# Gated projections in pieces behind one conditioning block each, and seven products per weight block for the values of latent and context

## The chip, the core and the metric

One core of a Trainium2 chip runs the whole program. Its engines work side by side: TensorE multiplies matrices, VectorE and ScalarE work element by element, GpSimd does what is left to it, SyncE issues most transfers from memory. The metric is the time of one execution on the device in microseconds. Everything is float32.

## What is computed

Two transformer layers in a row over 256 tokens of width 1024. The change lies at the start of the first. Cut to what matters there:

```python
mod_lat = silu(c)     @ w_ada + b_ada          # conditioning, 6 x 1024 columns
mod_ctx = silu(c_ctx) @ w_ada + b_ada
u_ctx = h_ctx * (1 + csc_m) + csh_m            # 256 tokens of context
u_lat = h_lat * (1 + sc_m) + sh_m              # 256 tokens of latent
k_c, v_c = split(u_ctx @ w_in[:, K_OFF:G_OFF])             # k 1024, v 2048 columns
q, k, v, g, glu, gates = split(u_lat @ w_in)
# q and k are turned by rope; o = retention of q over k, v and over k_c, v_c in both directions
za, zb = split(glu); z = za * sigmoid(zb)      # gated projection, then a convolution of 31 taps
z = silu(layernorm(depthwise_conv(z)))
mix = (sigmoid(ga) * (silu(g) * head_norm(o)) @ w_ret_out + sigmoid(gb) * (z @ w_conv_out)) @ w_mix_out
h = layernorm(ALPHA * h_lat + gt_m * mix)      # then experts, then the second layer
```

## The kernel before, in words

Activations lie with the width on the 128 partitions and the tokens along the free dimension: `uT` (latent) and `ucT` (context) are eight tiles of 128x256. Weights come in blocks of 1024 rows by 512 columns, 2048 KB, into eight bays. Three bays are the `ring`; the others are tensors that are free at the time: RA, Vc, KQ, ZC, and `extra` with a bit of uT. `make_jobs` lists the loads and the TensorE jobs of each block; a load waits until the last job on its bay is done, and `ROUNDS` and `EARLY_BAYS` say which bay is next. SyncE issues the loads in this order, one after the other.

At the start come four conditioning blocks (`ada`). For each, TensorE multiplies the two conditioning vectors by it (L783), VectorE copies the row (L1296), TensorE turns it to columns (L840) and VectorE adds the bias (L1267, L1271). Matmuls that compute nothing (L821) stand in the gaps. `ADA_FIRST` sets the order so that two blocks give the shift and the scale of half of the width. ScalarE (`modulate`, L510) and VectorE (L1303) then make `uT`. The first gated block is a `deep_job` (L832), whose sum runs over the width in the outer loop; the other three are ordinary jobs (L794). Their results go to two PSUM buffers of four tiles each (`PP`, a "pair"), used in turn; ScalarE takes the sigmoid, VectorE multiplies (L1347) and writes `zpad`. After each of them VectorE does 16 taps of the convolution (`convolve`, L1333 for the first tap of a tile, L1335 for the rest), each on 128x256 elements, each behind a wait on the one before.

Then k for latent and context, q, and the rope on VectorE (L1356 to L1358). The values: for each of four weight blocks one job for the context and one for the latent, 2 x 8 matmuls of 512 columns each (L805), into a pair; VectorE adds the bias (`with_bias`, L1364), then does 16 taps. TensorE may be one job ahead. GpSimd issues the transfers of the bias rows (L476) and computes nothing there. The last tap is followed by a reduction over the channels (L1340). In the heads behind it, PSUM tensors `MB0` to `MB3` take the scores (L896) and the outputs (L910, L913), and eight more conditioning blocks are multiplied, one per head.

## Time and profile before

| | us |
|---|---|
| median of 3 runs (1511.61 to 1511.84) | 1511.73 |
| the profiled execution itself | 1514.14 |
| its span, first to last instruction | 1512.3 |
| TensorE busy | 1463.0 |
| VectorE busy | 490.9 |
| ScalarE busy | 226.7 |
| GpSimd busy | 17.8 |

How to read it: a busy time is the sum of an engine's instructions in the profiled execution, which has a time of its own, here 2.4 us above the median. A float32 matmul appears as two instructions ("passes"), so that 16 of them are 8 matmuls. Passes are pipelined: their own duration overlaps that of the next, and the spacing of starts is what one costs. PE is TensorE, PEld its load of stationary operands, DVE is VectorE, ACT ScalarE, POOL GpSimd, SP SyncE.

### The profile page before, as it was taken

The numbers are of one execution on the slowest core, as the hardware profiler recorded it, in microseconds if no ns is written. First come the engines' busy times: TensorE is split into PE (matmuls) and PEld (weight loads), VectorE is DVE, ScalarE is ACT, GpSimd is POOL, SyncE is SP. The second block draws the span as 40 slices with busy tenths as digits, with TensorE's granted clock in tenths as the row PEclk, the third lists the DMA queues.
The fourth block names the chain that finished last, engine by engine and source line by source line (L and its number), as shares of the span: only waits on it lengthen the run. The fifth ranks groups of instructions, "written<-read, shape, count | busy, mean of one in ns | idle before, by whom it ended". The sixth has DMA issues, their size and how long they took to land.

```text
span 1512.3 us, 19230 instructions
## 1 busy us (share of the span) xinstructions
PE 1463.0 (97%) x8282; PEld 941.3 (62%) x8282; DVE 490.9 (32%) x1060; ACT 226.7 (15%) x438; POOL 17.8 (1%) x38
## 2 busy tenths in 40 slices
PE   8999999999999999999999998999999999999996
PEld 6888644564688887555555444445788886455542
DVE  1637866643102135223222121214223252211122
ACT  1210300231213004201111010112121022111011
POOL 0000000000000010000000000000010000000000
PEclk9999999999999999999999999999999999999999
DMA  9623322583434486999999999997564747999985
GB/s 388 271 86 112 112 83 105 184 317 132 156 127 163 169 354 241 371 427 428 427 426 427 428 427 428 428 421 322 144 224 158 281 167 289 429 426 428 427 336 249
DMA packets 36184, 435.42 MB, mean 288 GB/s; under 512 B 4336, under 2 KB 5752, under 8 KB 9736
## 3 DMA queue, kind: packets, MB, share of 16 engines
q1 hardware_dynamic: 33264, 427.89, 69.6%
q0 software_dynamic: 1664, 4.52, 0.8%
q10 hardware_dynamic: 1176, 1.84, 0.8%
q8 instruction: 63, 1.03, 0.3%
q14 instruction: 17, 0.14, 0.0%
HBM read 431.61 MB, written 2.62 MB: 287 GB/s over the span
## 4 chain that ended last, share of the span: by engine, by line
PE 83%; DMA 15%; DVE 1%; issue 1%; ACT 0%; SPq 0%; POOL 0%; DVEq 0%; POOLq 0%
PE PP L794 26%; PE PP L1069 17%; PE PP L805 12%; PE PP L1084 9%; PE MB L1053 5%; DMA ZC<-in_w_moe 5%; PE PP L832 4%; DMA RA<-in_w_moe 2%; DMA ring<-in_w_moe 2%; DMA Vc<-in_w_moe 2%; DMA uT<-in_w_moe 2%; PE PP L1045 1%; DMA Vc<-in_w_ada 1%; PE MB L910 1%; PE PP L783 1%; PE MB L896 1%
## 5 line engine op out<-in xcount | busy, mean ns | idle before, releaser
L794 PE MATMUL PP<-uT,ring 128*128 128x256 f32 x960 | 208.8, 379 | 0.0
L794 PEld LDWEIGHTS PP<-uT,ring 128*128 128x128 f32 x960 | 182.0, 190 | 25.1 <-issue 0.5
L805 PE MATMUL PP<-ring,uT 128*128 128x512 f32 x288 | 125.1, 593 | 0.0
L1335 DVE SCALAR_TENSOR_TENSOR ZC<-ZC,vec 128x256 f32<-128x256 f32 x240 | 116.4, 485 | 8.6
L1069 PE MATMUL PP<-ring,const 128*64 128x256 f32 x992 | 112.1, 380 | 5.1 <-DMA ring<-in_w_moe 4.8
L1053 PE MATMUL MB<-V 64*128 64x512 f32 x400 | 112.4, 640 | 1.7 <-DVE V L1718 0.9
L1697 DVE TENSOR_SCALAR V<-V 128x1 f32<-128x1 f32 x50 | 7.7, 154 | 309.2 <-PE PP L1069 309.2
L1069 PEld LDWEIGHTS PP<-ring,const 128*64 128x64 f32 x992 | 72.2, 137 | 49.0 <-issue 11.6
L805 PEld LDWEIGHTS PP<-ring,uT 128*128 128x128 f32 x288 | 54.4, 190 | 67.6 <-issue 67.6
L1712 DVE SCALAR_TENSOR_TENSOR V<-V 128x256 f32<-128x256 f32 x100 | 48.5, 485 | 108.7 <-PE MB L1053 94.0
L1084 PE MATMUL PP<-ring,const 128*64 128x512 f32 x336 | 76.7, 598 | 0.1
L658 ACT ACTIVATE V<-PP 128x256 f32<-128x256 f32 x50 | 19.2, 383 | 379.3 <-PE PP L1069 379.3
L1069 PE MATMUL PP<-ZC,const 128*64 128x256 f32 x512 | 58.3, 380 | 6.5 <-DMA ZC<-in_w_moe 6.3
L1069 PE MATMUL PP<-RA,const 128*64 128x256 f32 x512 | 58.3, 380 | 4.1 <-DMA RA<-in_w_moe 3.9
L662 ACT ACTIVATE const<-small 128x512 f32 x50 | 31.8, 636 | 168.2 <-PE PP L1069 167.8
L805 PE MATMUL PP<-ring,RA 128*128 128x512 f32 x128 | 55.6, 592 | 0.0
L794 PE MATMUL PP<-Vc,ring 128*128 128x256 f32 x256 | 55.6, 379 | 0.0
L1069 PEld LDWEIGHTS PP<-ZC,const 128*64 128x64 f32 x512 | 36.6, 137 | 29.1 <-DMA ZC<-in_w_moe 9.0
L1069 PEld LDWEIGHTS PP<-RA,const 128*64 128x64 f32 x512 | 36.6, 137 | 28.5 <-DMA RA<-in_w_moe 8.4
L794 PEld LDWEIGHTS PP<-Vc,ring 128*128 128x128 f32 x256 | 48.6, 190 | 6.6
L1084 PEld LDWEIGHTS PP<-ring,const 128*64 128x64 f32 x336 | 22.3, 136 | 47.0 <-issue 45.1
L1053 PEld LDWEIGHTS MB<-V 64*128 64x128 f32 x400 | 30.3, 184 | 30.4 <-issue 30.1
(399 smaller groups left out, 1641.9 us busy)
## 6 DMA issues: line engine op xcount, KB each, us to landing
ring<-in_w_moe SPq DMA_DIRECT2D x54, 2048.0 KB, 18.7
RA<-in_w_moe SPq DMA_DIRECT2D x22, 2048.0 KB, 16.0
ZC<-in_w_moe SPq DMA_DIRECT2D x22, 2048.0 KB, 17.4
KQ<-in_w_moe SPq DMA_DIRECT2D x18, 2048.0 KB, 18.7
Vc<-in_w_moe SPq DMA_DIRECT2D x17, 2048.0 KB, 18.4
extra<-in_w_moe SPq DMA_DIRECT2D x17, 1792.0 KB, 16.5
ring<-in_w_ada SPq DMA_DIRECT2D x11, 2048.0 KB, 8.4
ring<-in_w_gates SPq DMA_DIRECT2D x7, 2048.0 KB, 7.8
```

Of the source, the lines that this page charges most:

```text
L658: nc.scalar.activation(sg, bank[0][:, 0:L], ACT.Silu).then_inc(m["sg_ready"], 1)
L662: nc.scalar.activation(xs, xsc[:, :, bass.ds(at, SLOTS)], ACT.Copy).then_inc(m["xs_ready"], 1)
L783: ins = pe.matmul(out[at:at + 32, 0:2, :].rearrange("p a n -> p (a n)"), x, W[:, k * 512:(k + 1) * 512], start=k < 4 and late <= 0, stop=k ...
L794: ins = pe.matmul(out[:, c, :], W[:, k * width + at:k * width + at + P], X[:, k, :], start=k == 0, stop=k == K - 1)
L805: ins = pe.matmul(out[:, 2 * t:2 * t + 2, :].rearrange("p a n -> p (a n)"), X[:, k, t * P:(t + 1) * P], W[:, k * 512:(k + 1) * 512], start ...
L832: ins = pe.matmul(out[:, c, :], W[:, k * 512 + c * P:k * 512 + (c + 1) * P], X[:, k, :], start=k == 0 and c % 2 == 0, stop=k == DT - 1 and ...
L896: ins = pe.matmul(out[:, m, :], keys[:, h, m * P:(m + 1) * P], qT[:, h, :], start=True, stop=True)
L1053: ins = pe.matmul(acc[t][g], S[rows, t * P:(t + 1) * P], ys[rows, :], start=first, stop=done == "acc_done", tile_position=(SLOTS * g, 0))
L1069: ins = pe.matmul(bank[q][SLOTS * g:SLOTS * (g + 1), 0:L], x[:, k, :], weights(W, k * 512 + g * 256, 256), start=k == 0, stop=k == DT - 1, ...
L1084: ins = pe.matmul(bank[2][SLOTS * g:SLOTS * (g + 1), :], hts[:, c % 2, SLOTS * (c // 2):SLOTS * (c // 2 + 1)], weights(W, c * D + g * 512, ...
L1335: ins = V_.scalar_tensor_tensor(conv[:, t, :], zpad[:, t, k:k + L], tap, conv[:, t, :], ALU.mult, ALU.add)
L1712: linked(V_.scalar_tensor_tensor(Sk[:, c], placer[:, c], slotcol, weightr[:, c], ALU.is_equal, ALU.mult), k, c + 2)
```

## The change

Gated blocks 0 to 2 come in four pieces (`w_piece`), each with two of the eight width tiles of all three blocks, 1536 KB. The columns of the first four conditioning blocks are put in another order, so that block b gives shift and scale of width tiles 2b and 2b + 1. Behind conditioning block b these two tiles of `uT` are made, one by ScalarE and one by VectorE, and `glu_piece` adds their part to the sums of all three gated blocks, which stay open in both pairs and in MB2 and MB3. The conditioning rows use MB0 and MB1. The fourth gated block is one job as before. The context is loaded when the pieces are done.

The values of latent and context are one product of a 2 x 2 matrix (latent or context by halves of the width) with a 2 x 2 matrix (halves of the width by halves of the block's columns). `seven_products` computes it by seven products of quarters in place of eight. Five sums of quarters of the inputs are made once, five sums of quarters of the weights for each block, all on GpSimd. The results go to MB0 to MB3 in turn, and VectorE adds each to one or two quarters of V and Vct (`add_product`). Between the products VectorE does 3 or 4 taps; two taps and the reduction are left for the time behind the first g block. Bay 0 holds the weight sums, so that the value blocks come into bays 1 and 2 alone.

```diff
@@ make_jobs
-ADA_FIRST = (0, 2, 1, 3)
-EARLY_BAYS = (0, 1, 2, 4, 5)
+PIECES = 4
+EARLY_BAYS = (0, 1, 0, 1, 2, 4, 5, 3, 0, 1, 2, 0, 1, 2, 1, 2, 1)
+SUM_BAY = 0
...
-    order = (("mix1", (("ada", 4, ["ada"]), ("glu", 4, ["cm8"]), ("k", 2, ["cm8", "cm8c"]),
-                       ("q", 2, ["cm8"]), ("v", 4, ["tm8c", "tm8"]), ("ada", 8, ["ada"]), ("g", 4, ["tm8"]), ("gates", 4, ["cm8"]),
+    order = (("mix1", (("ada", 4, ["ada"]), ("piece", PIECES, []), ("glu", 4, ["cm8"]), ("k", 2, ["cm8", "cm8c"]),
+                       ("q", 2, ["cm8"]), ("v", 4, ["seven"]), ("ada", 8, ["ada"]), ("g", 4, ["tm8"]), ("gates", 4, ["cm8"]),
...
+        u_sums = [kw, Pc] + [extra[:, D * i:D * (i + 1)].rearrange("p (a n) -> p a n", a=4) for i in range(3)]
+        w_sums = [ring[:, SUM_BAY, D * i:D * (i + 1)].rearrange("p (a n) -> p a n", a=4) for i in range(4)] + [raw]
...
+        def quarters(b):
+
+            W = bays[loads[J["v", b, 0]["w"]]["bay"]].rearrange("p (k n) -> p k n", n=512)
+            return W[:, 0:4, 0:256], W[:, 0:4, 256:512], W[:, 4:8, 0:256], W[:, 4:8, 256:512]
+        lat1, lat2, ctx1, ctx2 = uT[:, 0:4, :], uT[:, 4:8, :], ucT[:, 0:4, :], ucT[:, 4:8, :]
@@ GpSimd
+            pool.wait_ge(u_ready, PIECES + 1)
+            pool.wait_ge(u_second, PIECES)
+            for out, x, y, op in zip(u_sums, (ctx1, lat1, lat1, ctx1, lat2), (ctx2, lat2, ctx2, lat1, ctx2),
+                                     (ALU.add, ALU.add, ALU.add, ALU.subtract, ALU.subtract)):
+                nc.gpsimd.tensor_tensor(out, x, y, op).then_inc(sums_made, 1)
+            job_wait(pool, J["q", 0, 0])
+            for b in range(4):
+                w_wait(pool, J["v", b, 0]["w"])
+                B11, B12, B21, B22 = quarters(b)
+                for i, (x, y, op) in enumerate(((B12, B22, ALU.subtract), (B21, B11, ALU.subtract), (B11, B22, ALU.add),
+                                                (B11, B12, ALU.add), (B21, B22, ALU.add))):
+                    if b:
+                        seven_wait(pool, b - 1, i + 2)
+                    elif i == 4:
+                        pool.wait_ge(rope_done, 4)
+                    nc.gpsimd.tensor_tensor(w_sums[i], x, y, op).then_inc(sums_made, 1)
@@ TensorE
+            def glu_piece(q, b):
+
+                if b == 0:
+                    w_wait(pe, piece[q])
+                    pe.wait_ge(u_ready, q + 1)
+                    pe.wait_ge(u_second, q + 1)
+                W = bays[loads[piece[q]]["bay"]]
+                for k in (2 * q, 2 * q + 1):
+                    for c in range(4):
+                        at = (2 * b + k % 2) * 512 + c * P
+                        ins = pe.matmul(glu_at(b, c), W[:, at:at + P], uT[:, k, :], start=k == 0 and c % 2 == 0,
+                                        stop=k == DT - 1 and c % 2 == 1)
...
-            deep_job(J["glu", 0, 0], uT, {0: first_half, 4: second_half})
-            for b in range(1, 4):
-                job(J["glu", b, 0])
+            for q in range(PIECES):
+                glu_piece(q, 0)
+                if q + 1 < PIECES:
+                    first_ada(q + 1)
+                glu_piece(q, 1)
+                if q + 1 < PIECES:
+                    turn_ada(q + 1)
+                glu_piece(q, 2)
+            job(J["glu", 3, 0])
...
+            def seven_products(b):
+
+                B11, _, _, B22 = quarters(b)
+                made = len(u_sums) + len(w_sums) * b
+                for p, (x, y, sums) in enumerate(((u_sums[0], B11, 1), (u_sums[1], B22, 2), (lat1, w_sums[0], made + 1),
+                                                  (ctx2, w_sums[1], made + 2), (u_sums[2], w_sums[2], made + 3),
+                                                  (u_sums[3], w_sums[3], made + 4), (u_sums[4], w_sums[4], made + 5))):
+                    n = 7 * b + p
...
+                    pe.wait_ge(sums_made, sums)
+                    if n >= 4:
+                        pe.wait_ge(seven_kept, n - 3)
+                    for t in range(LT):
+                        for k in range(4):
+                            ins = pe.matmul(MB[n % 4][:, t, :], x[:, k, t * P:(t + 1) * P], y[:, k, :], start=k == 0, stop=k == 3)
@@ VectorE
-            for h in range(2):
-                decay(h)
-                context_decay(h)
+            def add_product(b, p):
...
+                if p < 2:
+                    dve.wait_ge(bias_full[b % 2], 16 * (b // 2 + 1))
+                    plus, minus = ((ctx[0], bias[0]), (ctx[1], bias[1])) if p == 0 else ((lat[1], bias[1]), (lat[0], bias[0]))
+                    V_.tensor_tensor(plus[0], M, plus[1], ALU.add)
+                    ins = V_.scalar_tensor_tensor(minus[0], M, -1.0, minus[1], ALU.mult, ALU.add)
+                else:
+                    for out in ((lat[1], ctx[1]), (ctx[0], lat[0]), (lat[0], ctx[1]), (ctx[1],), (lat[0],))[p - 2]:
+                        ins = V_.tensor_tensor(out, out, M, ALU.add)
+                say(dve, ins, seven_kept, n + 1)
+            step = 9 * A_JOB
             for b in range(4):
-                with_bias(J["v", b, 0], b, Vct[:, :, b * 512:(b + 1) * 512])
-                convolve((9 + 2 * b) * A_JOB, (10 + 2 * b) * A_JOB)
-                with_bias(J["v", b, 1], b, Vt[:, :, b * 512:(b + 1) * 512])
-                convolve((10 + 2 * b) * A_JOB, (11 + 2 * b) * A_JOB)
+                for p in range(7):
+                    add_product(b, p)
+                    taps = 3 if p < 2 or b == 3 and p > 4 else 4
+                    convolve(step, step + taps)
+                    step += taps
+                if b < 2:
+                    for h in range(2):
+                        (decay, context_decay)[b](h)
...
+                if b == 0:
+                    convolve(step, DT * TAPS)
```

TensorE at the start of the program, before. `sT` holds the conditioning vectors; the line numbers are those of the kernel before:

```order
L783 MATMUL PP<-ring,sT 32x512 x8
L840 MATMUL PP<-lead,small 128x2 x4
L821 MATMUL MB<-V 128x128 x5
L783 MATMUL PP<-Vc,sT 32x512 x8
L840 MATMUL PP<-lead,small 128x2 x4
L821 MATMUL MB<-V 128x128 x6
L832 MATMUL PP<-uT,KQ 128x256 x32
L794 MATMUL PP<-uT,ring 128x256 x128
```

These are the third and the fourth conditioning block, then the first gated block; the last row is the other three gated blocks and k's first job. The same engine and place in the changed kernel, from the first conditioning block on (L906 is the conditioning job, L914 the turning, L928 a piece, L858 an ordinary job):

```order
L906 MATMUL MB<-ring,sT 32x512 x8
L885 MATMUL MB<-V 128x128 x3
L914 MATMUL MB<-lead,small 128x2 x4
L885 MATMUL MB<-V 128x128 x6
L928 MATMUL PP<-uT,ring 128x256 x8
L906 MATMUL MB<-ring,sT 32x512 x8
L928 MATMUL PP<-uT,ring 128x256 x8
L914 MATMUL MB<-lead,small 128x2 x4
L928 MATMUL MB<-uT,ring 128x256 x8
L928 MATMUL PP<-uT,Vc 128x256 x8
```

The gated matmuls now begin behind the first conditioning block, and each later conditioning job and turning stands between two of them. VectorE in the value stage before, one block of the four (L1364 adds the bias, L1335 and L1333 are taps):

```order
L1364 TENSOR_TENSOR V<-PP,biasr 128x2x512
L1335 SCALAR_TENSOR_TENSOR ZC<-ZC,vec 128x256 x16
L1364 TENSOR_TENSOR Vc<-PP,biasr 128x2x512
L1335 SCALAR_TENSOR_TENSOR ZC<-ZC,vec 128x256 x8
L1340 TENSOR_REDUCE rs<-ZC 128x256
```

The same in the changed kernel, the first five products of a block (L1498 and L1499 start the values with the bias, L1502 adds, L1431 and L1429 are taps):

```order
L1498 TENSOR_TENSOR Vc<-MB,biasr 128x2x256
L1499 SCALAR_TENSOR_TENSOR Vc<-MB,biasr 128x2x256
L1431 SCALAR_TENSOR_TENSOR ZC<-ZC,vec 128x256 x3
L1498 TENSOR_TENSOR V<-MB,biasr 128x2x256
L1499 SCALAR_TENSOR_TENSOR V<-MB,biasr 128x2x256
L1431 SCALAR_TENSOR_TENSOR ZC<-ZC,vec 128x256 x3
L1502 TENSOR_TENSOR V<-V,MB 128x2x256
L1502 TENSOR_TENSOR Vc<-Vc,MB 128x2x256
L1431 SCALAR_TENSOR_TENSOR ZC<-ZC,vec 128x256 x4
```

In place of one addition of 1024 elements for 16 taps there are one or two of 512 for 3 or 4 taps. GpSimd in the changed kernel, where before only the transfers of the bias rows stood (L516 makes sums of the inputs, L527 of the weights):

```order
L508 DMA biasr<-in_bias_rows 128x512 x2
L516 ISA
L516 TENSOR_TENSOR small<-RA 128x1024
L516 TENSOR_TENSOR small<-uT 128x1024
L516 TENSOR_TENSOR extra<-uT,RA 128x1024
L516 TENSOR_TENSOR extra<-RA,uT 128x1024
L516 TENSOR_TENSOR extra<-uT,RA 128x1024
L527 TENSOR_TENSOR ring<-ring 128x1024 x4
L527 TENSOR_TENSOR small<-ring 128x1024
```

Five sums of the inputs come first, then five of the first weight block; the row of four and the one behind it come three more times.

## Rows read from the trace of the kernel before

**Rows 1.** The page, busy us with share and instructions, and the granted clock.

```profile
PE 1463.0 (97%) x8282; PEld 941.3 (62%) x8282; DVE 490.9 (32%) x1060; ACT 226.7 (15%) x438; POOL 17.8 (1%) x38
...
PEclk9999999999999999999999999999999999999999
```

**Rows 2.** The chain of waits, first 300 us: start us, us, what.

```profile
2.60 20.73 DMA Vc<-in_w_ada
...
29.99 14.05 PE PP L832 x64
44.05 124.32 PE PP L794 x576
168.37 109.87 PE PP L805 x256
278.23 1.74 PE MB L896 x8
...
280.10 0.69 DVE small L1410
280.79 0.61 DVE small L1412
```

**Rows 3.** Order of time, conditioning stage: start, us, engine, line, operation [idle before].

```profile
9.11 1.92 PE L783 MATMUL PP<-ring,sT 128*32 128x512 f32 x16 [1.71 <-DMA ring<-in_w_ada]
...
11.17 0.69 DVE L1296 COPY small<-PP 128x512 f32<-128x512 f32 x1 [11.17 <-PE PP L783]
...
11.91 1.05 PE L840 MATMUL PP<-lead,small 128*128 128x2 f32 x8 [0.88 <-DVE small L1296]
...
13.07 0.23 DVE L1267 TENSOR_TENSOR modT<-PP,lead 128x4 f32<-128x4 f32 x2 [1.22 <-PE PP L840]
...
14.12 1.92 PE L783 MATMUL PP<-ring,sT 128*32 128x512 f32 x16
...
28.90 0.17 DVE L1271 TENSOR_SCALAR modT<-modT 128x8 f32<-128x8 f32 x1
29.11 1.09 ACT L510 ACTIVATE uT<-hT,modT 128x256 f32<-128x256 f32 x2 [0.80 <-DVE modT L1271]
```

**Rows 4.** Order of time, context on ScalarE and the first gated block on VectorE.

```profile
45.25 4.04 ACT L510 ACTIVATE RA<-RA,modT 128x256 f32<-128x256 f32 x8 [6.85 <-DMA RA<-in_ctxT]
...
51.59 0.88 DVE L1347 SCALAR_TENSOR_TENSOR ZC<-PP,vec,small 128x256 f32<-128x256 f32 x2 [9.24 <-ACT small L528]
```

**Rows 5.** Busy time in the value stage: stretch, its length, each engine, clock, DMA.

```profile
168.20:278.20 110.00, 110.00 (x258) 48.77 (x257) 75.97 (x133) 10.04 (x17) 1.61 (x3) 1.00 0.23 84
```

**Rows 6.** Order of time, VectorE in the value stage.

```profile
177.99 0.75 DVE L1381 SCALAR_TENSOR_TENSOR small<-const,lgs 128x512 f32<-128x512 f32 x1
...
184.31 0.69 DVE L1387 TENSOR_TENSOR small<-small 128x512 f32<-128x512 f32 x1 [0.35 <-ACT small L565]
184.92 1.22 DVE L1364 TENSOR_TENSOR Vc<-PP,biasr 128x1024 f32<-128x1024 f32 x1
...
197.19 8.30 DVE L1335 SCALAR_TENSOR_TENSOR ZC<-ZC,vec 128x256 f32<-128x256 f32 x16
...
270.02 3.67 DVE L1340 TENSOR_REDUCE rs<-ZC 128x256 f32<-128x2048 f32 x1
```

**Rows 7.** Order of time, the one GpSimd operation on tensors, at the span's end.

```profile
1507.87 1.26 POOL L497 TENSOR_TENSOR Kc<-Kc,uT 128x512 f32<-128x512 f32 x1 [342.77 <-ACT Kc L765]
```

**Rows 8.** What writes Kc at the end: durations ns min/median/max, first and last start.

```profile
L1770 DVE SCALAR_TENSOR_TENSOR Kc<-MB,biasr,uT x3: 742/742/752, 1507.0 to 1508.4; 128x512 f32<-128x512 f32 x3
```

**Rows 9.** Order of time, the second late conditioning block on TensorE.

```profile
290.66 1.92 PE L783 MATMUL PP<-ring,sT 128*32 128x512 f32 x16
```

**Rows 10.** DMA issues, 230 to 350 us: count, KB each, median us to landing.

```profile
ring<-in_w_ada SPq DMA_DIRECT2D x7, 2048.0 KB, 8.1
```

More of the change, by code:

```diff
@@ L112, in make_jobs @@
             first = sum(x["src"] == src for x in loads)
-            for b in ADA_FIRST if src == "ada" and not first else range(first, first + count):
+            for b in range(first, first + count):
                 for half, kind in enumerate(kinds):
                     jobs.append(dict(src=src, b=b, kind=kind, half=half, w=len(loads), i=len(jobs), pair=dense % 2, use=dense // 2))
-                    dense += src != "ada" or b < 4 or b == 11
-                loads.append(dict(src=src, b=b, bay=bay_of(phase)))
+                    dense += (src != "ada" or b == 11) and (src, b) != ("glu", 2) and src != "v"
+                    if src == "glu" and b < 3:
+                        jobs[-1]["w"] -= 1
+                if src != "glu" or b == 3:
+                    loads.append(dict(src=src, b=b, bay=bay_of(phase)))
         experts(n)
     last_of = {j["w"]: j["i"] for j in jobs}
+    pieces = [w for w, x in enumerate(loads) if x["src"] == "piece"]
+    last_of |= {w: last_of[pieces[-1]] for w in pieces}
     for w, x in enumerate(loads):
@@ L122, in make_jobs @@
         x["nth"], x["prev"] = len(before), before[-1] if before else None
+    last_v = next(w for w, x in enumerate(loads) if (x["src"], x["b"]) == ("v", 3))
+    next(x for x in loads[last_v + 1:] if x["bay"] == SUM_BAY)["prev"] = last_v
     return jobs, {(j["src"], j["b"], j["half"]): j for j in jobs}, loads, last_of
@@ L346, in tail_bays, with glu_at, seven_wait @@
             return [order[(done + q) % len(order)] for q in range(3)]
+        piece = [w for w, x in enumerate(loads) if x["src"] == "piece"]
+        def glu_at(b, c):
+            return MB[2 + c // 2][:, c % 2, :] if b == 2 else PP[J["glu", b, 0]["pair"]][:, c, :]
+        def seven_wait(eng, b, p):
+            if p == 6:
+                eng.wait_ge(job_done, J["v", b, 0]["i"] + 1)
+            else:
+                eng.wait_ge(seventh, 6 * b + p + 1)
+        def quarters(b):
+            W = bays[loads[J["v", b, 0]["w"]]["bay"]].rearrange("p (k n) -> p k n", n=512)
+            return W[:, 0:4, 0:256], W[:, 0:4, 256:512], W[:, 4:8, 0:256], W[:, 4:8, 256:512]
+        lat1, lat2, ctx1, ctx2 = uT[:, 0:4, :], uT[:, 4:8, :], ucT[:, 0:4, :], ucT[:, 4:8, :]
         def job_wait(eng, j):
@@ L407, in _ @@
             sp.dma_start(lead[:, :], a["lead"]).then_inc(ld_c, 16)
-            for w in range(4):
-                load(w)
-            sp.dma_start(hT[:, :, :], a["xT"]).then_inc(ld_x, 16)
-            for half, done in enumerate((ld_glu, w_full[loads[4]["bay"]])):
-                h = slice(half * BLK // 2, (half + 1) * BLK // 2)
-                sp.dma_start(bays[loads[4]["bay"]][:, h], a["w_glu"][0, :, h]).then_inc(done, 16)
+            load(0)
+            sp.dma_start(hT[:, 0:2, :], a["xT"][:, 0:2, :]).then_inc(ld_x, 16)
+            load(piece[0])
+            load(1)
+            sp.dma_start(hT[:, 2:8, :], a["xT"][:, 2:8, :]).then_inc(ld_xs, 16)
+            load(piece[1])
+            load(2)
+            load(piece[2])
+            load(3)
+            load(piece[3])
             sp.dma_start(vec[:, :], a["vec"]).then_inc(ld_vec, 16)
-            sp.wait_ge(w_full[loads[2]["bay"]], 16)
+            load(8)
             sp.dma_start(row[:, :], a["rows"].partition_broadcast(P)).then_inc(ld_rest, 16)
             sp.dma_start(const[:, :], a["const"]).then_inc(ld_rest, 16)
-            load(5)
+            load(9)
+            job_wait(sp, J["glu", 2, 0])
             sp.dma_start(ctxT, a["ctxT"]).then_inc(ld_ctx, 16)
-            for w in range(6, at[0]):
-                if w == 8:
+            for w in range(10, at[0]):
+                if w == 12:
                     sp.dma_start(wr[0][:, :, :], a["wr0"]).then_inc(ld_wr, 16)
@@ L538, in raw_copy @@
                 else:
-                    act.wait_ge(pair_free[1], J["glu", 3, 0]["use"] + 1)
+                    last = J["glu", 3, 0]
+                    act.wait_ge(pair_free[last["pair"]], last["use"] + 1)
                 for i in range(4):
@@ L781, in job @@
                         at, late = 32 * (k % 4), j["b"] - 4
[L782 to L784 removed]
+                        ins = pe.matmul(out[at:at + 32, 0:2, :].rearrange("p a n -> p (a n)"), sT[:, k, 8 - late:40 - late],
+                                        W[:, k * 512:(k + 1) * 512], start=k < 4 and late == 0, stop=k >= 4 and late == 7,
+                                        tile_position=(0, at))
                 elif kind in ("cm8", "cm8c", "cm4", "cm16"):
@@ L876, in _ @@
                 job(J["k", b, 0])
[L877 removed]
+                pe.wait_ge(u_ready, PIECES + 1)
                 job(J["k", b, 1])
```

157 lines of the change are left out of this document (88 added, 69 removed).

## The prediction

> **What bounds the kernel now.** I read the page's busy shares first, then the chain of waits of the first 300 us, the order of time on each engine around it, and the DMA issues. TensorE is busy 97% of the span, at a granted clock of 9 tenths or more in every slice [rows 1] and 1.00 in the value stage [rows 5], so the higher of its two levels, 2.4 GHz. In the chain [rows 2] the reader is to see two parts. Until 29.99 us the conditioning blocks come in by DMA and TensorE has next to nothing to do. From there to 278.2 us there is only TensorE: 14.05 us for the first gated block, nine jobs of 124.32 / 9 = 13.81 us (three gated, four k, two q), eight value jobs of 109.87 / 8 = 13.73 us. So a piece of TensorE work taken away here is worth its time, as long as VectorE (busy 75.97 of 110 us in the value stage [rows 5]) and the transfers keep up. The kernel after 278 us is the same program; its loads are released by TensorE's jobs and move with them.
>
> **Part 1, gated projections in pieces.** Before, TensorE computes nothing of the projections until all four conditioning blocks have come, 2048 KB each, one per 14.12 - 9.11 = 5.01 us [rows 3]. The change puts a quarter of the rows' depth of three gated blocks (1536 KB) behind each conditioning block. At 2.5 us per 1024 KB: the first block lands at 9.1 us as now, x's first two tiles at 9.7, piece 0 at 13.5, conditioning block 1 at 18.5, and each further pair 8.8 us later (a little more at first, for the rest of x: 20.4).
>
> TensorE: conditioning job 0 ends at 9.1 + 1.92 = 11.0; copy 0.69 (+0.14), turning 1.05, VectorE's sum 0.23 and 0.17 with their gaps, then one tile modulated on ScalarE in 1.09 / 2 = 0.55 [rows 3]: about 14.2, behind piece 0. One (piece, block) is 16 passes, 13.81 / 4 = 3.45 us, so TensorE works to 17.7 and waits until 18.5. From there I find no wait: conditioning jobs 1 to 3 at 1.87, eleven more quarter jobs 38.0, three turnings at 0.93 (their spacing in the dense stretch), the fourth gated block 13.8: 18.5 + 5.6 + 38.0 + 2.8 + 13.8 = 78.7. Conditioning block 2 is asked for at about 31.7 and lands at 29, block 3 at 45.5 and lands at 38: from the second piece on the margin grows. Before, the same point is 44.05 + 3 x 13.81 = 85.5. **Gain 6.7 us.** If the transfers came 20% slower the loss would be at the first two waits only, about 3 us.
>
> What is late next: VectorE. Gated block 0 now finishes at 58 (after the last piece), not 44, then come four rounds of 0.88 + 16 taps of 0.519 = 9.2 us [rows 4, 6]. Block 3 leaves PSUM at 87.4; the first context job of k needs that buffer at 78.7 + 13.8 = 92.5. Margin 5 us. The context is asked for after the pieces (it lies where piece 3 lay): 65 + 5 + 4.04 us on ScalarE [rows 4] = 74, needed at 92.5. So T, the start of the value stage, goes from 168.4 to 161.7.
>
> **Part 2, seven products.** Removed: 8 jobs, 109.87 us. Added: 4 x 7 products of 2 x 4 matmuls of 256 columns, 16 passes each: 28 x 3.45 = 96.7 us. TensorE alone gains 13.1 us. The additions that pay for it lie on two other engines.
>
> VectorE: 20 products have two additions out of PSUM, 8 have one. No row shows this form at 512 elements on V; the nearest is L1410 with L1412 behind it, 0.69 and then 0.61 [rows 2]; half of the 1024-element form, 1.22 / 2 = 0.61, is the lower end and 0.75 (L1381) the upper [rows 6]. I take 0.69 + 0.61 + 0.04 = 1.34 for two, 0.73 for one: 32.6 us. Taps 102 x 0.519 = 52.9, four decay steps and two sums 4.5. Together 90.0 us. A product has 1.34 + 4 x 0.519 = 3.42 us of VectorE against 3.45 of TensorE. That is no slack at all, but VectorE may lag four products (n waits for n - 4). It comes free at T + 9.6 (the rope ends at 177.96 [rows 6]), so product 0 leaves at T + 11.0 and is needed at T + 13.8; by the same count the margin stays above 2 us through the stage. At the end VectorE is at T + 9.6 + 90.0 = T + 99.6, plus 0.69 for the first score operation = T + 100.3. Before it was 280.79 - 168.37 = T + 112.4 [rows 2]. So 1.1 of the 13.1 us are given back and **12.1 us** gained; at the lower end of the addition 1 us more, at the upper 2.5 less.
>
> GpSimd: 5 sums of the inputs and 20 of weight quarters, 128x1024 each. The only such row is L497, 1.26 us for 512 elements [rows 7]. Bounds: 1.26 if all of it were fixed, 2.52 if it goes with the size; I take 2.4. Five per block are 12 us of its 24.2, and every sum may start when the product that used it last is over, a block ahead: hidden, unless one took over 4.8 us. The first four for block 0 have 13.8 + 6.9 us for 9.6.
>
> What these sums do to VectorE beside them is the one open price, since no row shows a GpSimd operation that reads beside a VectorE operation with two tensors out of SBUF, which a tap is. Bounds: nothing, and the whole of each sum, 2.4 us. The nearest row is L1770, three operations of 742, 742 and 752 ns, of which the latter two ran beside L497 [rows 7, 8], so at nothing or 0.01 us. I take nothing. It is a near row, not an equal one: L1770 takes one tensor from PSUM.
>
> On this the Trainium skill speaks against the change. "SBUF — State Buffer", section "Who interferes with whom", says that a VectorE instruction with two SBUF inputs contends with a GpSimd one that reads SBUF, and that whichever is first keeps the shared ports for its whole length, while one with a single SBUF input is left alone. L1770 agrees with the second half; on the first no row here bears. By it the sum is that of rival A.
>
> Elsewhere: in the heads behind the values, conditioning load 2 of the late eight is now asked for at the stage's end and not a block earlier (its bay holds the weight sums). It lands in 8.1 us and is used 290.66 - 278.23 = 12.4 us in [rows 2, 9, 10]: free; without those 4 us it would cost what is missing. The last two taps and the reduction, 1.0 + 3.67 us [rows 6], move behind the first g block, where a job of 13.73 us of TensorE covers them beside two operations of 1.22 us.
>
> **Sum.** The profiled execution took 1514.14 us with a span of 1512.3. 6.7 + 12.1 = 18.8 off, with 0.8 put back for the additions' upper end: 1496.1 for it. It stood 2.4 us above the median of the runs, so **1493.7 us** for that.
>
> **Rivals.**
> A. Each sum stops VectorE for its whole length. Price: the four sums before T fall on rope and taps, 9.6 us; of the stage's 90 us of VectorE work 57.4 (64%) read two tensors from SBUF, so the 16 other sums cost between 0.64 x 38.4 = 24.6 and 38.4 us, take 31.5. The end is T + 141.4, 29 us later than before. In part 1 the five input sums, 12 us, exceed the margin of 5 us: TensorE waits 7 us for the PSUM buffer, which eats its gain. Together +29 us: **1541**. For it: a tap has two SBUF tensors, and VectorE has no slack. Against it: only that the near row shows nothing. It decides from 18.8 / 20 = 0.94 us per sum upward: below that the kernel is still faster.
> B. In between: the two engines slow each other for part of the time, 0.3 to 1.2 us per sum. 20 x that against 18.8: 1499 to 1517, take **1506**.
> C. The change doesn't reach what it says: the stage's pace is set by VectorE because the additions take 1.5 and 0.8 us with their waits. 20 x 0.16 + 8 x 0.07 = 3.8 us: **1498**. Nothing in the rows speaks for it.
>
> **How the numbers follow.** Forecast, with C as its edge: 0.42 (1490 to 1499). B 0.20, of it 0.10 faster, 0.03 the same, 0.07 slower. A 0.34 (1525 to 1555), since what speaks against it is a row of another form. A late transfer or another stall of over 19 us: 0.04, slower. Faster 0.52, same 0.03, slower 0.45; within 0.2% (3 us) a measurement can't tell a change from none. The likeliest case is 1493.7, its own range 1490 to 1499; the range of 8 in 10 has to reach into A: 1490 to 1543.
>
> **What would show it.** Part 1: TensorE dense from 18.5 us, one wait before it, fourth gated block over at 78.7; wrong if it waits for a piece or for PSUM at 92. Part 2: 448 passes at 0.216 us in 97 us without a wait for VectorE's additions. The taps beside GpSimd's sums: 485 ns in the forecast, some of them 2.5 us and more in A, where TensorE's waits name the additions. The score stage starts at about T + 97 in the forecast, past T + 130 in A. The forecast is wrong if the taps' mean rises above some 0.6 us.

## The result, and the profile after

The changed kernel takes **1538.03 us** (median of 4 runs, 1537.36 to 1538.96) against 1511.78 for the kernel before (4 runs, 1511.61 to 1513.39). The ratio is 1.017, with a 95% interval of 1.0157 to 1.0183: slower by 26 us. The forecast of 1493.7 was wrong, and so was its direction. The time that came is near that of rival A, 1541; the wide range of 1490 to 1543 holds it only because it was stretched to reach into A.

From the page of the changed kernel: busy us with share and instructions (as in [rows 1]), then the shares of each engine in the chain of work that ended last, then the row of the taps (busy us and mean ns behind the first bar).

```profile
PE 1458.8 (95%) x8450; PEld 978.2 (64%) x8450; DVE 556.7 (36%) x1102; ACT 227.4 (15%) x438; POOL 79.0 (5%) x63
...
PE 70%; DMA 14%; DVE 14%; issue 1%; ACT 0%; SPq 0%; POOL 0%; DVEq 0%; POOLq 0%
...
L1431 DVE SCALAR_TENSOR_TENSOR ZC<-ZC,vec 128x256 f32<-128x256 f32 x240 | 154.2, 643 | 8.6
```

VectorE now holds 14% of the chain that ended last; before it was 1%. The taps have a mean of 643 ns; before it was 485, and 16 of them with their gaps took 8.30 us [rows 6]. A mean hides what happened; the spread of the same line does not (durations ns min/median/max):

```profile
L1431 DVE SCALAR_TENSOR_TENSOR ZC<-ZC,vec x240: 483/485/2725, 62.7 to 382.8; 128x256 f32<-128x256 f32 x120
```

The median tap is what it was. A few take five times as long. The chain of waits in the first block of the value stage (start us, us, what) shows which, with GpSimd's order of time in the same stretch under it:

```profile
189.48 0.69 DVE Vc L1498
190.17 0.61 DVE Vc L1499
190.78 0.02 issue
190.81 1.37 DVE ZC L1431
192.18 0.02 issue
192.20 2.47 DVE ZC L1431
194.67 0.02 issue
194.69 2.46 DVE ZC L1431
197.16 0.02 issue
197.18 0.69 DVE V L1498
197.87 0.61 DVE V L1499
```
```profile
189.53 2.35 POOL L527 TENSOR_TENSOR small<-ring 128x1024 f32<-128x1024 f32 x1 [21.67 <-DVE KQ L1457]
191.84 5.03 POOL L527 TENSOR_TENSOR ring<-ring 128x1024 f32<-128x1024 f32 x2
197.58 2.35 POOL L527 TENSOR_TENSOR ring<-ring 128x1024 f32<-128x1024 f32 x1 [0.72 <-PE MB L980]
```

GpSimd's sum of 189.53 to 191.88 runs beside two additions out of PSUM (L1498, L1499), which take 0.69 and 0.61 us, as costed. The tap that starts at 190.81 ends only at 192.18, 0.30 us after the sum. The next two taps take as long as the next two sums (5.03 us for both). In these rows a sum stops a tap, which reads only SBUF, and leaves alone an addition that reads PSUM beside one SBUF tensor, which is what L1770 was [rows 8].

Where TensorE then waits (start us, us, ..., in brackets the idle time before and what ended it), in part 1, in the value stage and in front of the second head's scores:

```profile
20.34 1.92 PE L906 MATMUL MB<-ring,sT 128*32 128x512 f32 x16 [2.44 <-DMA ring<-in_w_ada]
...
67.07 26.28 PE L858 MATMUL PP<-uT,ring 128*128 128x256 f32 x121
...
100.33 16.17 PE L858 MATMUL PP<-RA,ring 128*128 128x256 f32 x64 [5.47 <-DVE ZC L1443]
...
171.59 7.07 PE L980 MATMUL MB<-ring,small 128*128 128x256 f32 x32
...
190.92 6.58 PE L980 MATMUL MB<-ring,extra 128*128 128x256 f32 x16 [5.36 <-DVE Vc L1499]
...
297.74 1.10 PE L997 MATMUL MB<-KQ,Kc 128*128 128x256 f32 x4 [0.57 <-DVE Vc L1502]
...
305.71 2.05 PE L997 MATMUL MB<-KQ,Kc 128*128 128x256 f32 x4 [6.01 <-DVE small L1532]
```

The busy time of each engine around the wait of 5.47 us in front of the k context job, and in the value stage (stretch, length, busy us of PE, PEld, DVE, ACT and POOL, granted clock, DMA share, GB/s):

```profile
93.00:100.00 7.00, 1.86 (x9) 1.30 (x7) 6.53 (x15) 0.00 (x0) 0.00 (x0) 0.84 0.00 0
100.00:104.00 4.00, 3.67 (x9) 2.98 (x10) 3.71 (x9) 3.68 (x6) 0.00 (x0) 0.50 0.02 4
...
108.00:112.00 4.00, 4.00 (x20) 3.53 (x19) 0.44 (x1) 0.00 (x0) 0.00 (x0) 1.00 0.00 0
...
186.00:200.00 14.00, 7.97 (x23) 6.28 (x24) 13.75 (x11) 3.36 (x5) 9.68 (x4) 0.76 0.00 1
```

The wait in front of the k context job cost more than its length: behind its 5.47 us the granted clock is 0.50 for about four us, so TensorE, which had been busy for 1.86 of the 7 us before, runs at the lower level of 1.2 GHz there, and a job whose row reads 13.98 in other places reads 16.17. In the value stage VectorE is busy 13.75 of 14 us and TensorE 7.97.

The account in us of the profiled executions, at three marks: the value stage starts at 171.59 and not 168.37 (+3.2). The second head's scores, which wait for VectorE's two score operations, start 134.12 after that (305.71 - 171.59) and not 113.17 after (281.54 - 168.37): +20.95. The first job of the gates' stage starts at 364.51 and not 338.55: +26.0, of which the last 1.8 lie behind the last wait, where the granted clock is low. (The operation that [rows 2] puts at T + 112.4, the first of the two, ends in the changed kernel at T + 133.4.) From there on the two kernels take about the same: the medians less these marks are 1538.03 - 364.51 = 1173.5 and 1511.78 - 338.55 = 1173.2, the profiled executions themselves 1537.36 - 364.51 = 1172.9 and 1514.14 - 338.55 = 1175.6.

### The profile page after: what moved, and what is told of

Read it like the earlier page. It is cut to its first block, busy times and chain, and to the rows that moved or that the text cites. A ratio compares the mean times of both kernels' runs of the same rounds, so it can differ in the third digit from the quotient of the medians.

```text
span 1535.5 us, 19672 instructions
## 1 busy us (share of the span) xinstructions
PE 1458.8 (95%) x8450; PEld 978.2 (64%) x8450; DVE 556.7 (36%) x1102; ACT 227.4 (15%) x438; POOL 79.0 (5%) x63
## 3 DMA queue, kind: packets, MB, share of 16 engines
q1 hardware_dynamic: 33408, 427.89, 68.5%
## 4 chain that ended last, share of the span: by engine, by line
PE 70%; DMA 14%; DVE 14%; issue 1%; ACT 0%; SPq 0%; POOL 0%; DVEq 0%; POOLq 0%
PE PP L858 20%; PE PP L1169 16%; DVE ZC L1431 9%; PE PP L1184 9%; PE MB L1153 5%; PE PP L869 4%; DMA ZC<-in_w_moe 4%; PE PP L896 3%; DMA RA<-in_w_moe 2%; DMA Vc<-in_w_moe 2%; DMA ring<-in_w_moe 2%; DMA uT<-in_w_moe 2%; PE PP L928 1%; PE PP L1145 1%; DMA ring<-in_w_ada 1%; PE MB L1010 1%
## 5 line engine op out<-in xcount | busy, mean ns | idle before, releaser
L858 PE MATMUL PP<-uT,ring 128*128 128x256 f32 x832 | 181.2, 379 | 0.0
L858 PEld LDWEIGHTS PP<-uT,ring 128*128 128x128 f32 x832 | 157.7, 190 | 21.8 <-issue 0.5
L1431 DVE SCALAR_TENSOR_TENSOR ZC<-ZC,vec 128x256 f32<-128x256 f32 x240 | 154.2, 643 | 8.6
L1153 PE MATMUL MB<-V 64*128 64x512 f32 x400 | 112.4, 640 | 1.7 <-DVE V L1842 0.9
L869 PE MATMUL PP<-ring,uT 128*128 128x512 f32 x160 | 69.5, 593 | 0.0
L858 PE MATMUL PP<-Vc,ring 128*128 128x256 f32 x256 | 55.6, 379 | 0.0
L869 PEld LDWEIGHTS PP<-ring,uT 128*128 128x128 f32 x160 | 30.1, 190 | 37.0 <-issue 37.0
L858 PEld LDWEIGHTS PP<-Vc,ring 128*128 128x128 f32 x256 | 48.6, 190 | 6.6
L1840 DVE TENSOR_TENSOR V<-PP,uT 128x512 f32<-128x512 f32 x32 | 22.1, 692 | 80.4 <-PE PP L1184 80.4
```

Of the source, the lines that this page charges most:

```text
L858: ins = pe.matmul(out[:, c, :], W[:, k * width + at:k * width + at + P], X[:, k, :], start=k == 0, stop=k == K - 1)
L869: ins = pe.matmul(out[:, 2 * t:2 * t + 2, :].rearrange("p a n -> p (a n)"), X[:, k, t * P:(t + 1) * P], W[:, k * 512:(k + 1) * 512], start ...
L1153: ins = pe.matmul(acc[t][g], S[rows, t * P:(t + 1) * P], ys[rows, :], start=first, stop=done == "acc_done", tile_position=(SLOTS * g, 0))
L1431: ins = V_.scalar_tensor_tensor(conv[:, t, :], zpad[:, t, k:k + L], tap, conv[:, t, :], ALU.mult, ALU.add)
L1840: ins = V_.tensor_tensor(ys, bank[2], gate_row, ALU.mult)
```

## The experiments

The first job of the gates' stage (the first g block, L869 in the changed kernel) is used as the mark, "first gates job". Kernels whose values are not the reference's (e1, e2, e3, e9, e10) can send other rows to other experts later on, so their totals are not compared (e1 takes 1158.1 us behind the mark, the changed kernel 1173.5). Four theories are told apart: P, that a GpSimd operation which reads SBUF stops a VectorE operation with two SBUF tensors; Q, that VectorE simply had too much to do (in e5, that the first stage is late for another reason); R, that TensorE or the additions out of PSUM set the pace of the value stage; S, that the one-input form of a tap is stopped by anything GpSimd does.

All kernels in one table, times in us, interval of 95%. A ratio is taken to runs of the kernel before made beside that experiment (medians 1511.78 to 1513.86), not to the first row. The longest tap is that of the 240 taps behind the first of each tile. The marks are of one profiled execution each and carry what its start did: the fourth gated block starts at 66.33 (e4), at 67.0 to 67.3 (changed, e2, e3, e5, e9) or at 68.5 to 68.9 (the others), mostly because the granted clock from 20 to 24 us is 0.57 to 0.69 in these last and 1.00 in the rest. Differences of marks below some 2.6 us say nothing.

| kernel | median | ratio to before | 2nd head's scores | first gates job | longest tap |
|---|---|---|---|---|---|
| before | 1511.78 | 1 | 281.54 | 338.55 | 0.49 |
| changed | 1538.03 | 1.017 (1.0157 to 1.0183) | 305.71 | 364.51 | 2.73 |
| e1 sums only write | 1483.71 | 0.980 (0.978 to 0.982) | 266.96 | 325.60 | 0.49 |
| e2 sums of one input | 1493.41 | 0.986 (0.985 to 0.988) | 274.70 | 333.54 | 1.34 |
| e3 taps of one input | 1519.80 | 1.0045 (1.0031 to 1.006) | 286.80 | 346.58 | 2.52 |
| e4 pieces only | 1509.65 | 0.998 (0.9967 to 0.9998) | 276.36 | 333.38 | 0.49 |
| e5 input sums late | 1529.84 | 1.0116 (1.0099 to 1.0133) | 297.98 | 357.20 | 2.67 |
| e6 value taps later | 1510.32 | 0.998 (0.9974 to 0.9993) | 281.75 | 338.77 | 2.66 |
| e7 both, and k/q taps | **1495.40** | **0.988 (0.9865 to 0.9899)** | 265.77 | 322.79 | 2.53 |
| e8 sums on VectorE | 1527.43 | 1.0083 (1.0066 to 1.01) | 296.16 | 355.22 | 2.53 |
| e9 half sums | 1508.00 | 0.996 (0.9946 to 0.9975) | 274.64 | 333.46 | 1.52 |
| e10 e1 with e3's taps | 1497.30 (one run) | - | 266.00 | 324.64 | 1.20 |
| e11 e4 with unused sums | 1527.07 | 1.0079 (1.0057 to 1.01) | 293.57 | 352.65 | 7.73 |

**e1, GpSimd's sums only write.**

```diff
-nc.gpsimd.tensor_tensor(w_sums[i], x, y, op).then_inc(sums_made, 1)
+nc.gpsimd.memset(w_sums[i], 0.0).then_inc(sums_made, 1)
```
(and the input sums likewise)

> Each of GpSimd's 25 sums is a fill of the same output with zero: it writes 1024 elements and reads nothing, so the values are not computed. Theory P (a GpSimd operation that reads SBUF stops VectorE operations with two SBUF tensors): no tap above 0.5 us, TensorE never waits at the k context job or in the value stage, 1511.8 - 4.5 (start) - 12.1 (value stage) = about 1495 us. Theory Q (the added additions alone make VectorE too slow, and the trace's long taps are a matter of records): stays above 1530.

The durations of the same taps, and TensorE's only wait between 60 and 300 us:

```profile
L1431 DVE SCALAR_TENSOR_TENSOR ZC<-ZC,vec x240: 483/485/487, 64.5 to 343.9; 128x256 f32<-128x256 f32 x120
```
```profile
266.96 2.04 PE L997 MATMUL MB<-KQ,Kc 128*128 128x256 f32 x4 [2.87 <-DVE small L1532]
```

None of the two-input taps is long, neither the stall at 94.9 nor those of the value stage are there, and the first gates job comes 38.9 us before the changed kernel's and 13.0 before that of before. The schedule itself is faster; all of the loss, and more, is what the sums do. Theory Q falls: 90 us of work in the stage were not too much. One thing was not as P had it. The first tap of each tile (L1429) reads one tensor, and two of the eight took 1.58 and 1.25 us beside a write:

```profile
L1429 DVE TENSOR_SCALAR ZC<-ZC,vec x8: 412/414/1581, 64.0 to 241.7; 128x256 f32<-128x256 f32 x8
```

**e2, sums of one input** (`tensor_scalar(w_sums[i], x, 1.0, None, ALU.mult)`).

> Each sum is a copy of its first input by GpSimd (times 1.0): one tensor read, so the values are not computed. Theory P: still a reader, each stops VectorE for its own length; at 1.0 to 1.3 us apiece 20 x 1.1 x 0.8 = 18 us of the value stage come back: 1508 to 1515, longest taps about 1.6 us. If it takes two reads of GpSimd to disturb: 1495, taps at 0.485.

The expectation missed on both sides. GpSimd's copy takes 2.77 us, longer than the sum, and yet the longest tap beside it is 1.34 us in all. VectorE's loss from 150 to 300 us is 130 taps at a mean of 549 ns in place of 485 (8.3 us), 1.3 us on the decay steps and 0.7 on the first taps: 0.5 us for each of the 20. The changed kernel loses 139 x (683 - 485) = 27.5 us on its taps and 6 on four decay operations: 33.5, or 1.7 each. So a reader of one tensor disturbs too, for much less than its own length; why, no run shows.

**e3, taps of one input.**

```diff
-V_.scalar_tensor_tensor(conv[:, t, :], zpad[:, t, k:k + L], tap, conv[:, t, :], ALU.mult, ALU.add)
+V_.tensor_scalar(conv[:, t, :], zpad[:, t, k:k + L], tap, col("conv_b", t), ALU.mult, ALU.add)
```

> Every tap of the convolution reads only the padded input and not the running sum, so the convolution is left out; GpSimd's sums are as in the change. Theory P: taps 0.41 us throughout, beside the sums too, since they have one SBUF tensor: about 1494. If any VectorE operation were stopped by a reading GpSimd: taps of 2.4 us stay and the time is 1530 or more.

```profile
L1431 DVE TENSOR_SCALAR ZC<-ZC,vec x240: 411/414/2515, 62.8 to 364.8; 128x256 f32<-128x256 f32 x120
```

The expectation missed: these taps read one SBUF tensor and take 414 ns alone, but beside a sum up to 2.52 us all the same. VectorE loses some 31 us on them and on 11 other operations from 150 to 300 us (130 taps at 609 ns in place of 414 are 25.3), nearly as much as in the changed kernel. The first gates job comes 18 us earlier, about what 240 taps that are 0.07 us shorter give. "Two tensors out of SBUF" was therefore not the whole condition.

**e10, both edits of e1 and e3 together**, to ask what stops the one-input form.

> Edit: GpSimd's 25 additions only write zeros, and each tap reads one tensor (multiply and add with two columns) in place of two; the values are not the reference's. With sums that only write, the two-tensor taps never took over 487 ns, but 2 of the 8 one-tensor taps there took 1.58 and 1.25 us. Theory S (the one-tensor form is stopped by anything that GpSimd does, for its length): median tap 412 to 414 ns, and where one lies beside a write of 0.95 us it takes 1.2 to 1.6 us, so about one long tap for each of the 25 writes that falls on a tap. Theory P as it stood (only a GpSimd operation that reads stops VectorE; the two long ones had another cause): no tap over 0.45 us. The first gates job does not tell them apart (322 to 327 by both).

```profile
L1431 DVE TENSOR_SCALAR ZC<-ZC,vec x240: 411/414/1201, 64.4 to 342.8; 128x256 f32<-128x256 f32 x120
```

With two-input taps a writing GpSimd stopped none of 240 (487 at most). With one-input taps it does, up to 1.20 us, and the 131 taps from 150 to 300 us have a mean of 492 ns in place of 414: theory S, as far as sums and writes go. The two forms are stopped by different things: of those tried, the two-input one only by a GpSimd operation that reads, the one-input one also by one that only writes.

**e9, half of each sum** (128x512 added, the other half set to zero).

> Edit: each of GpSimd's 25 sums is made over half of its elements (128x512), and the other half is filled with zeros, so that the values are not the reference's. Theory P with a stop as long as the addition: additions of 1.2 to 1.3 us, the longest taps 1.2 to 1.4 us in place of 2.5 to 2.7, VectorE's loss in the value stage 12 to 16 us in place of 33.5, no or hardly a stall before the k context job, second head's scores at 284 to 292, first gates job 342 to 350. If a stop costs the same whatever the length (a hand-over price), the longest taps stay at 2.4 us and the first gates job after 358. The total is not to be compared behind the experts, since other values are routed.

```profile
L1435 DVE SCALAR_TENSOR_TENSOR ZC<-ZC,vec x240: 483/485/1515, 63.0 to 351.7; 128x256 f32<-128x256 f32 x120
```

The sums take 1.27 to 1.57 us, the longest tap 1.52. The longest stop goes with the length of the sum; a fixed hand-over price of the size seen before is out. VectorE loses 10.0 us from 150 to 300, 0.5 per sum. The expected place of the first gates job was too late by 9 us: I had scaled the loss of the end, but only what exceeds VectorE's slack gets there.

**e4, the gated pieces alone**, with the value stage of before (eight jobs, no sums).

> Part 1 of the change alone: pieces at the start, values by eight jobs as before, GpSimd computes nothing. By the trace of the change, where the fourth gated block ends at 81.0 in place of 85.5: 1511.8 - 4.5 = 1507.3. By the forecast's own sum (78.7): 1505. If the transfers set the start and later work gives it back: 1511.8.

The first gates job is 5.2 us earlier than that of before; part 1 was costed at 6.7. In whole executions the gain is smaller and hardly clear of the noise: e4's ten runs spread from 1506.55 to 1514.99, their median of 1509.65 is 2.1 us below 1511.78, and the ratio's interval ends at 0.9998. The profiled execution was the fastest of the ten.

**e11, the suspected cost by itself**: e4, with 20 sums on GpSimd whose results nobody reads.

```diff
+for part, j in enumerate((J["v", b - 1, 1] if b else J["q", 0, 0], J["v", b, 0])):
+    job_wait(pool, j)
...
+    for i in range(3 - part):
+        nc.gpsimd.tensor_tensor(u_sums[2 + i], lat1, lat2, ALU.add).then_inc(sums_made, 1)
```

> Edit: the suspected cost by itself. The kernel with the gated projections in pieces but the value stage of before (eight jobs of its own, 1509.65 us, first gates job at 333.38), and in its value stage GpSimd makes 20 additions of 128x1024 whose results nobody uses, three behind each even job and two behind each odd one. Nothing waits for them. Theory P: VectorE is as full as TensorE in that stage, each addition holds one tap for 2.45 us in place of 485 ns, unless it falls on an operation that reads PSUM; 20 additions cost 28 to 40 us: first gates job 361 to 374, total 1537 to 1550. Theory Q (what slowed the changed kernel was its seven products and their additions, not GpSimd): first gates job 333 to 336, total 1508 to 1514.

Order of time of e11, GpSimd and VectorE in the same stretch, and the chain there:

```profile
202.28 12.20 POOL L512 TENSOR_TENSOR extra<-uT 128x1024 f32<-128x1024 f32 x5
```
```profile
201.44 19.58 DVE L1416 SCALAR_TENSOR_TENSOR ZC<-ZC,vec 128x256 f32<-128x256 f32 x16
```
```profile
201.44 0.50 DVE ZC L1416
...
201.96 7.73 DVE ZC L1416
209.69 0.03 issue
209.71 2.52 DVE ZC L1416
212.24 0.03 issue
212.26 2.51 DVE ZC L1416
```

Sixteen taps take 19.58 us in place of 8.30 [rows 6]: 2.26 per sum. One tap is held through three sums in a row. Nothing uses what these sums make, the bias rows that GpSimd fetches behind them are not waited for (VectorE is idle 0.1 us in all before its four additions to V, and as little before those to Vc), and the kernel is 17.4 us slower than e4. The first gates job comes 19.3 later, of which 2.5 were there before the first sum (the fourth gated block starts at 68.87 and not 66.33), so the sums cost some 17 us. That is less than expected. VectorE lost 44 us (179 taps at 709 ns, and 4 us elsewhere), but in the value stage of before it had been idle 34.6 of 112 us, with waits of about 4.2 us in front of most jobs' outputs. The slack took over half of it. Theory Q falls here too.

**e5, the input sums later.**

```diff
 pool.wait_ge(u_second, PIECES)
+last_glu = J["glu", 3, 0]
+pool.wait_ge(pair_free[last_glu["pair"]], last_glu["use"] + 1)
```

> Edit: GpSimd makes the four input sums (two 128x1024 additions each in the first gated stage of the changed kernel) only after the last gated block's PSUM buffer has been read. Theory P (each reading GpSimd addition stops VectorE's two-tensor operations for its length): the 15 taps that stand before the last gated block take 7.8 us again instead of 18.1, the PSUM buffer for the k context job is free in time, the 5.5 us stall of TensorE at 94.9 and the 2.2 us at the lower clock behind it are gone; the same additions now fall beside the k and q taps, where VectorE has slack. First score matmul 5 to 8 us earlier than in the changed kernel (298 to 301 against 305.71), total 1530 to 1533. Theory Q (the rest of the first stage is late for another reason, such as the late first transfer): the k context job stalls all the same, total 1536 to 1539.

(There are five input sums, not four.) The k context job starts at 94.95 without a wait and takes 13.98 us; the value stage starts at 164.0 and not 171.6. So the 5.5 us stall and its 2.2 us of lower clock came from the five input sums (8.2 us off the median).

**e6, the value stage's taps behind it**, 16 behind each of the first three g blocks and the rest behind the fourth.

```diff
 add_product(b, p)
-taps = 3 if p < 2 or b == 3 and p > 4 else 4
-convolve(step, step + taps)
-step += taps
...
-if b == 0:
-    convolve(step, DT * TAPS)
+convolve(step, step + 16 if b < 3 else DT * TAPS)
+step += 16
```

> Edit: the 56 or so taps that the changed kernel runs between its seven products per block go behind the value stage, 16 behind each of the first three blocks of the gates' stage and the rest behind the fourth; all work is kept. Theory P: in the value stage VectorE has 62 us of its own work and up to 16 stops that now mostly have no two-tensor operation to stop, so TensorE is dense there. Without its stalls the stage from 171.8 ends at about 277 instead of 299, and the first score matmul comes at 281 to 286 (the stall of the first stage stays, some 7 us against the kernel whose additions only write, which began it at 266.96). First gates job 340 to 344, total 1512 to 1518. Theory R (the pace of the value stage is set by TensorE's own clock or by the additions from PSUM, not by the taps): first score matmul after 295, total above 1528.

All twenty weight sums are still made, and from the second block on TensorE has no wait (28 products, one wait of 5.35 us in the first block). Theory R falls: the additions out of PSUM, with the sums beside them, do not hold the products up. 27.7 us off the median. By itself e6 does not part the stops from the work of the taps, which left the stage too; e1 does that.

**e7, e5 and e6, and 32 of the k and q taps moved too.**

> Edit: both of the above together, and of the taps that stand beside the k and q projections 32 fewer there, which also go behind the gates' blocks. All work is kept. Theory P: neither the k context stall nor the value stage's stalls; first score matmul at 266 to 272, first gates job 324 to 330, then 1492 to 1498 in all unless the taps that were moved (about 100 of 485 ns, 49 us) now end after the gates' stage, which would give back up to 5 us. Theory R as before: above 1520.

TensorE in the value stage of e7, and VectorE and GpSimd (columns as above), and its first products and the second head's scores:

```profile
165.00:200.00 35.00, 35.00 (x164) 30.82 (x163) 18.37 (x23) 10.15 (x17) 14.63 (x7) 1.00 0.35 128
200.00:262.00 62.00, 62.00 (x289) 54.59 (x288) 22.82 (x33) 0.00 (x0) 24.50 (x12) 1.00 0.21 77
```
```profile
165.62 7.07 PE L982 MATMUL MB<-ring,small 128*128 128x256 f32 x32
...
265.77 1.10 PE L999 MATMUL MB<-KQ,Kc 128*128 128x256 f32 x4 [1.57 <-DVE small L1529]
```

GpSimd makes every sum (16 of the 20 in the stage, 39 us with its three transfers), each as long as in the changed kernel, and TensorE is busy 97.0 of 97 us. The wait of 5.35 us that e6 still had in its first block is gone too. All work is kept. **1495.4 us: 1.2% faster than before and 2.8% faster than the changed kernel.** The last moved tap starts at 428.7, and that costs nothing that can be seen: behind the first gates job the kernel takes 1495.4 - 322.79 = 1172.6 us, as the others do.

**e8, the weight sums on VectorE itself**, all taps where the change put them.

```diff
+def weight_sum(b, i): ...
+    V_.tensor_tensor(w_sums[i], x, y, op).then_inc(sums_made, 1)
...
 add_product(b, p)
+if b < 3 and p > 1:
+    weight_sum(b + 1, p - 2)
```

> Edit: the twenty sums of weight quarters (128x1024 each) are made by VectorE itself, five before the value stage and the others behind the products; GpSimd makes only the five input sums, where it did, and all taps stay where they are. Theory P: VectorE takes 15 more operations of 1.22 us in the value stage (the time of the additions of that size that it makes beside an idle GpSimd), 18.3 us on top of 90.0, but every tap takes 485 ns, so that the stage ends near T+112 and not T+125, with T at 171 as in the changed kernel (the stall of the first stage stays): score stage's second head at 288 to 294, first gates job 346 to 353, total 1519 to 1526, faster than the changed kernel by 12 to 19 us although VectorE does more. Theory Q (VectorE was simply too full and a sum costs it nothing beside): VectorE gets 18 us more to do, first gates job after 375, total above 1548.

VectorE makes 20 more operations of 1.22 us, 24.5 us more work, and the kernel is 10.6 us faster than the changed one. Its own 1.22 us per sum are cheaper than the 1.7 that a sum on GpSimd took from it. The first gates job comes 2 us later than the range that was expected: the stage did take VectorE 107.8 us (188.31 to 296.1), as counted (90.0 + 18.3), but I let it enter at T + 9.6, and the backlog of part 1 and the first five sums made that T + 15.5.

## Why the prediction was wrong

**The step that failed** is "I take nothing" for what GpSimd's sums do to VectorE beside them. It rested on L1770, the nearest row, which takes one tensor from PSUM. The prediction said that this row is not an equal one, and that the Trainium skill speaks against it, and then took the row's value for the forecast. What it took for nothing measured 1.7 us per weight sum, 33.5 us in all. e1 against the changed kernel (38.9 us at the first gates job) and e11 against e4 (19.3 us, some 17 of them the sums') show that the sums cost the time; the rows at 189.48 to 197.16 show its condition.

**Rival A was right in mechanism and nearly in size.** It said 41.1 us for 20 weight sums and VectorE's end at T + 141.4. The end came at T + 133.4, 33.1 later than the forecast's T + 100.3, and the excess summed from the rows is 33.5. Of this 8.2 fell on the four taps before T (2.67, 2.48, 2.47 and 2.47 us). The 16 others cost 25.3, the lower end of A's 24.6 to 38.4: sums beside additions out of PSUM were free. In part 1 A said 7 us of waiting; it was 5.47 and 16.17 - 13.98 = 2.2 at the lower clock. That A's total is off by only 3 us is in part luck: it had 29 us behind T, where 22.8 came, and nothing before it, where 3.2 came. Its condition, two tensors out of SBUF, is also too narrow, as e3 shows.

**Part 1's gain of 6.7 us** was mis-sized, not wrong. The second conditioning job started at 20.34 and not 18.5, because its block landed later; the fourth gated block was over at 67.07 + 13.8 = 80.9 and not 78.7. That is 4.6 earlier than before; e4, without any sum, has 5.2 at the first gates job. From 20.34 to 94.9 TensorE was dense, as forecast. Two slips of the sum change nothing here: 85.5 - 78.7 is 6.8 and not 6.7, and the prediction's own terms give 44.9 and not 45.5 for the time at which conditioning block 3 is asked for. The margin of 5 us before the k context job was right: it holds in e4 and e5 and is used up by the five input sums (15 taps in 18.14 us).

**Part 2's TensorE time** was right: 97 us from 165.62 to 262.31 in e7. VectorE's additions were right too (0.69 and 0.61), and so was GpSimd's 2.4 us per sum (2.35 to 2.64).

**Even without the stops** the forecast's 18.8 us were 5.8 too many: e1's first gates job stands 13.0 before that of before. Its value stage starts at 165.51 and not 161.7 (3.8: the late block, and the conditioning job behind that wait, which took 3.05 us in place of 1.92). In the profile of e1 that job ran at a granted clock of 0.64; in that of the changed kernel, at 1.00, the fourth gated block started 1.7 us earlier (67.07 and not 68.81). The second head's scores start at 266.96, T + 101.4, where the forecast means T + 101.0 (T + 100.3 and the second score operation) (0.4). TensorE waits 2.87 us for VectorE, and the granted clock is 0.61 from 266 to 270 us: from these scores to the first gates job e1 takes 58.6 us and the kernel before 57.0 (1.6).

**The threshold.** A was to decide from 0.94 us per sum. e9 and e2 lose 0.5 per sum and reach the first gates job 5.1 and 5.0 us before that of before; the changed kernel loses 1.7 and is 26 us after it. The sign changes between the two, which fits the prediction's count and does not show its number.

**Rivals B and C.** B's price, 0.3 to 1.2 us per sum, is that of other sums (e2, e9). C's longer additions are in no row.

**Elsewhere:** the late conditioning load cost nothing, since the heads, from the second head's scores to the first gates job, take 57.0 us in e7 as before the change (322.79 - 265.77 and 338.55 - 281.54). Nor did the last two taps and the reduction, since the time behind the first gates job is about the same.

## What to carry over

Before work is given to an idle GpSimd, list what VectorE runs beside it by where its inputs lie: here what read only SBUF was stopped for about the length of the sum, what read PSUM was not, and the price was near the sum's time where VectorE had no slack. Put such sums beside VectorE's PSUM work, or move the SBUF-only work out of the stage, before you give the sums up: here the same sums cost 26 us in one order and let the kernel gain 17 in another. And where the nearest row differs from the operation in just the property in doubt, it is no evidence for the cheap end of a range.

## What the runs showed of the hardware

- A one-input TENSOR_SCALAR tap out of SBUF (414 ns) was stopped by a GpSimd sum (2.52 us in e3) and even by GpSimd writes of 0.95 us (up to 1.20 in e10, 1.58 in e1). The two-input tap (485 ns) was not stopped by the write (487 at most in e1). The rule of the Trainium skill ("SBUF — State Buffer", section "Who interferes with whom") names both cases: two SBUF inputs contend with a GpSimd that reads, and operations that can enter a two-port mode contend with it; the prediction, which had one-input operations left alone, dropped the condition "outside the 2-port perf modes". That the one-input taps ran in such a mode is not shown; of its speed they show little, 414 ns against 485.
- "For its whole length" held for two-input sums. It did not for GpSimd's one-input operation in e2: that is 2.77 us long, and the longest tap beside it took 1.34.
- Sums that follow each other need not let a tap through between them: in e11 one tap took 7.73 us, three sums. In the changed kernel one tap ran per sum. By the profile's times that tap of e11 had started at 201.96, 0.32 us before the first sum (202.28) and behind a transfer that GpSimd issued at 201.70, and was held all the same. So these rows do not show that whichever is first keeps the ports; what decides it is open.
- GpSimd took 2.35 us for 128x1024 summed (up to 2.69 beside VectorE's taps), 1.27 for 128x512, and 0.95 to write 128x1024.
- Why the first transfers came 1.8 us later than their sizes say was not tried.
